# One scan per step in block 1's stick-breaking attention, and another spread of the top-k pieces of token tile 0

## The chip, the cores and the metric

The kernel runs on one core of a Trainium2 chip. The metric is the device time of one execution in microseconds. Three executions of the kernel before took 3242.63, 3243.86 and 3246.19 us; the median, 3243.86, is its time.

## What is computed

One decoder layer over 1024 tokens of width 1024, all in float32:

```
xn  = rmsnorm(x)
mix = (sigmoid(g_sb) * (stick_breaking(q, k, v) @ W_sb)
       + sigmoid(g_ml) * (mLSTM(conv_silu(q), conv_silu(k), v, i, f) @ W_ml)) @ w_out
h   = x + mix
y   = h + PEER(rmsnorm(h))
out = rmsnorm(y)
```

Stick-breaking attention has 8 heads of 64; for each query block of 128 tokens and each head it weighs all earlier keys with `w = exp(log_sigmoid(z) - suffix)`, where `suffix` is a reverse running sum of `softplus(z)` along the keys.

PEER picks, for each token and each of 8 query heads, 16 of 16384 experts: the 16 best of 128 scores in each of two halves, then the 16 best of the 256 sums. For its 128 experts a token needs the rows `u` and `v` (1024 floats each): `y = sum over experts of gate * gelu(u . x) * v`.

## The kernel before

**Blocks and tiles.** The mixer (everything up to `h`, and the expert queries and scores) works on 4 blocks of 256 tokens, b = 0 to 3. PEER works on 8 tiles of 128 tokens, i = 0 to 7; block b yields tiles 2b and 2b + 1. Block 0's mixer runs first. From then on the stream of expert rows is what the kernel is laid along.

**The stream.** Each tile has 128 experts per token, taken as 64 pairs, so there are 512 pairs (`slots`), counted on through the tiles; this text calls them pair 0 to 511. For each expert GpSimd issues one indirect DMA (`L1107`) that gathers 128 rows of `u` and `v` (8 KB a token, 1 MB in all) into one of `RS = 8` buffers of `rowsb`. VectorE takes the dot with `u` (`dot`, L1984), ScalarE the gelu (`gelu`, L1420), the gate (L1434) and a diagonal matrix (`spread`, L1439), and TensorE adds `diag * v` into `yacc` (`add_rows`, L1018, which signals `v_done`). GpSimd waits for `v_done` of the expert 8 back, that is of the pair four back, before it fills the buffer again.

**The mixer in steps.** Blocks 1 to 3 are written as Python generators, one for each engine, that are cut into the same steps: 3 of norm, 13 of the first projections (k, q, v of the attention), `n_sba(b)` of attention, 14 of the second projections (mLSTM), 29 of the mLSTM and the gates (`mix0` to `mix28`), 9 of the output, 3 of the second norm and 19 of the expert queries and scores. `steps[s][b]` says how many steps of block b follow pair s. On each engine the order in a pair s is fixed: TensorE does `add_rows`, then the steps; ScalarE `gelu`, `spread`, then the steps; VectorE the two dots, then the top-k pieces, then the steps. Each step on TensorE that projects takes one weight unit of 512 KB from a ring of three (`wt`); SyncE refills a place when TensorE has used it. The attention steps load nothing.

**The attention's steps.** A value v stands for a pair of heads and one of the two query blocks, 8 in all (`NV`), each with two heads h. `logits(v)` (TensorE, L792) makes z for both heads. `shares` (ScalarE, L1125 tanh and L1192) turns them into factors `rem`. `scan(v, h)` (VectorE, L1567 and L1570) makes the weights, `flip` (TensorE, L803) transposes them, `turn` (ScalarE, L1125) copies them to SBUF, `values(v)` (TensorE, L816) multiplies with v, and ScalarE keeps the result. Which of these a step k holds is told by `logits_at`, `scans_at`, `flips_at` and `values_at`. `sba(k)` on ScalarE does the `turn`s of the flips of step k - 1, then the `shares` of the logits of step k - 1, then keeps the y of step k. For blocks 0 and 1 (one group of keys) there are 12 steps: logits of value k, both scans and flips of value k - 2, values of k - 3. For blocks 2 and 3 (two groups) there are 20: one head's scan per step.

**Top-k.** The search for a tile's experts is cut into pieces, 9 for two heads (`top_parts`), which run on VectorE behind the dots. `parts_at[i][p]` gives the number after pair p of tile i; tile 0's last three groups and all of tile 1 are placed by the loop over n at L452 to L459. GpSimd waits for tile 0's last group of experts before it issues for pair 48, some four pairs ahead, and for those of tile 1 before pairs 64, 80, 96 and 112.

**The planner.** `steps` comes from `spread_ticks`: it goes through the pairs and places the next step of a block as long as the summed costs of TensorE, VectorE and DMA (estimates in the code, `load_of` and `slot_load`, a top-k piece at 1.75 us) don't run ahead of the time `each` of a pair, with at most two larger steps in a pair for block 1 and one for the others; `each` rises until all steps fit. Block 1's steps lie from pair 11 to pair 107. Before the change they are placed so: first projections to pair 25; `sba0` in 25, `sba1` and `sba2` in 26, then `sba3` in 27, none in 28, 4, 5, 6 in 29 to 31, none in 32, 7 and 8 in 33 and 34, none in 35, 9 to 11 in 36; second projections from 37 (`p2_1` in 38); `mix11` in 63, none in 64 and 65, `mix12` in 66; the last output steps in 89; the three norm steps in 90, 90 and 91 and the first query step in 91.

Of the kernel before, what the change touches and what calls it, by code (L numbers as in the profile page):

```python
# [66 lines left out]
def build(nc, xT, x, vecs, w_feat, w_if, w_tok, w_merge, w_out, w_query, keysT, uv, rows, out):  # L67
    ctx = ExitStack()
    with ctx:
# [203 lines left out]
        def key_groups(b):  # L273
            return (NT * b) // 4 + 1

        queries = [(hp, il) for hp in range(PAIRS) for il in range(NT)]
        NV = len(queries)


        def n_sba(b):  # L280
            return NV + 4 if key_groups(b) == 1 else 2 * NV + 4

        def logits_at(b, k):
            g_ = key_groups(b)
            return divmod(k, g_) if 0 <= k < NV * g_ else None

        def scans_at(b, k):
            if key_groups(b) == 1:
                return [(k - 2, 0), (k - 2, 1)] if 2 <= k < NV + 2 else []
            return [divmod(k - 3, 2)] if 3 <= k < 2 * NV + 3 else []  # L290

        def flips_at(b, k):
            return [(v, h, g) for v, h in scans_at(b, k) for g in range(key_groups(b))]

        def values_at(b, k):
            if key_groups(b) == 1:
                return k - 3 if 3 <= k < NV + 3 else None
            return (k - 5) // 2 if k >= 5 and k % 2 == 1 and (k - 5) // 2 < NV else None

# [8 lines left out]
        for b in range(NB):  # L308
# [7 lines left out]
            for k in range(n_sba(b)):  # L316
                if values_at(b, k) is not None:
                    put(("y", b, values_at(b, k)), own + 2)
                if logits_at(b, k):
                    for h in range(2):  # L320
                        put(("z", b) + logits_at(b, k) + (h,), own + h)
                for f, q in enumerate(flips_at(b, k)):
                    put(("flip", b) + q, own + 3 - f)
# [72 lines left out]
        def load_of(b):  # L396
            load = [(3.0, 0.0, 0.0), (5.6, 0.9, 0.0), (3.0, 0.0, 0.0)]
            load += [(UNIT_PE, 0.0, UNIT_DMA)] * len(PROJ1) + [(0.0, 0.0, 0.0)]
            for k in range(n_sba(b)):
                pe_, dve_ = 0.2, 0.2  # L400
                if logits_at(b, k):
                    pe_ += 0.9
                for v, h in scans_at(b, k):
                    dve_ += 0.3 + 3.2e-3 * (NT * b + queries[v][1] + 1) * P
                pe_ += 0.6 * len(flips_at(b, k))
                if values_at(b, k) is not None:
                    pe_ += 0.29 * (NT * b + queries[values_at(b, k)][1] + 1)
                load.append((pe_, dve_, 0.0))
# [27 lines left out]
        TOP_EACH, BLOCK_END = 9, 44  # L436
# [4 lines left out]
        N_PARTS = 4 * TOP_EACH  # L441


        parts_at = [[0] * PP for i in range(TT)]
# [7 lines left out]
        for n in range(83):  # L452
            i, p = divmod(n, PP)
            if n < 20:
                parts_at[i][p] = {0: 0, 1: 4, 2: 2, 3: 2, 4: 0, 5: 2, 6: 2, 7: 2}.get(n, 1)
            elif n < 40:
                parts_at[i][p] = (n - 19) * TOP_EACH // 20 - (n - 20) * TOP_EACH // 20
            else:
                parts_at[i][p] = (n - 39) * N_PARTS // 43 - (n - 40) * N_PARTS // 43  # L459


        def slot_load(s):
# [47 lines left out]
        with nc.Block() as block:  # L510

            @block.sync
            def _(sp):
# [45 lines left out]
                def mix(b):  # L559
# [19 lines left out]
                    for k in range(n_sba(b) if b > 0 else 0):  # L579
                        yield  # L580
# [936 lines left out]
            def _(dve):  # L1517
# [9 lines left out]
                def mix(b):  # L1527
# [45 lines left out]
                    def sba(k):  # L1573
                        if k == 0:
                            ready(dve, ("sbv", b, NT - 1))
                            mark(dve.memset(left[:, span:span + 1], 1.0))
                            settle()
                        for v, h in scans_at(b, k):
                            scan(v, h)
# [539 lines left out]
```

## Time and profile before

| | |
|---|---|
| median of three executions | 3243.86 us |
| profiled execution, its own time | 3241.54 us |
| its span | 3239.7 us |
| TensorE matmul busy | 2590.7 us (80%) |
| VectorE busy | 2075.6 us (64%) |
| ScalarE busy | 1130.4 us (35%) |
| GpSimd busy | 1209.7 us (37%) |
| DMA | 1259.44 MB, mean 389 GB/s, gathers 80.7% of 16 engines' span, weights and rest some 15% |
| granted TensorE clock, mean | 0.91 |

The page gives the span in 40 slices of 81 us, and for each the busy share of every engine, the granted clock and the DMA rate. The rate is below 285 GB/s in the first four, then between 385 and 420 in all but the last.

The chain of work that ended last goes to the gathers for 37% of the span, to TensorE for 35% and to VectorE for 10%. Matmuls are pipelined and the ends of their records are modelled, so a busy TensorE isn't one at its peak; the granted clock is 1 at 2.4 GHz and 0.5 at 1.2 GHz.

### The profile page before, as it was taken

Reading aid. Unit: us, or ns where it says so; the run is one execution under the profiler, and the core shown is the slowest. Engines: PE = TensorE matmul, PEld = TensorE weight load, DVE = VectorE, ACT = ScalarE, POOL = GpSimd, SP = SyncE. Lnnn points to the kernel's source line nnn. Section 1 sums busy time; section 2 is a strip of 40 time slices with the busy share of each in tenths; the row PEclk is TensorE's granted clock in tenths of the full one; section 3 lists DMA queues with packets and bytes.
Section 4 is the critical chain, followed back from the end, with each engine's and each line's share of the span. In section 5 each row is a group of like instructions: output and inputs, shape, how many; then the busy total and the mean of one; then the engine's idle time right before and its main releaser. Section 6 shows DMA issues by size and latency. Waiting matters only on the chain.

```text
span 3239.7 us, 40489 instructions
## 1 busy us (share of the span) xinstructions
PE 2590.7 (80%) x14564; PEld 1311.4 (40%) x14564; DVE 2075.6 (64%) x4816; ACT 1130.4 (35%) x3556; POOL 1209.7 (37%) x1048
## 2 busy tenths in 40 slices
PE   8999978998889788997787777998787555555555
PEld 6776535554455244553454333455253111111111
DVE  2325769686458887764448898775447857765444
ACT  2213345342232643332323464334222322232223
POOL 0002334333334453333334464334334443444443
PEclk9999999999999999999898999999998787777778
DMA  4467999999999999999999999999999999999998
GB/s 154 135 193 281 416 413 387 414 418 414 385 413 416 411 419 416 413 416 417 415 415 402 413 404 418 402 415 417 416 414 415 408 420 419 416 416 418 416 420 339
DMA packets 221367, 1259.44 MB, mean 389 GB/s; under 512 B 25328, under 2 KB 29424, under 8 KB 90096
## 3 DMA queue, kind: packets, MB, share of 16 engines
q0 software_dynamic: 147456, 1073.81, 80.7%
q1 hardware_dynamic: 66208, 162.61, 13.5%
q10 hardware_dynamic: 7504, 20.45, 1.6%
q8 instruction: 115, 1.88, 0.2%
q14 instruction: 84, 0.69, 0.1%
HBM read 1251.02 MB, written 5.77 MB: 388 GB/s over the span
## 4 chain that ended last, share of the span: by engine, by line
DMA 39%; PE 35%; DVE 10%; issue 6%; ACT 6%; POOL 3%; SPq 0%; POOLq 0%; DVEq 0%; ACTq 0%
DMA rowsb<-uv,e_idx 37%; PE yacc L1018 13%; PE mixp L641 8%; DVE rowsb L1984 5%; PE mixp L666 4%; POOL rowsb L1107 3%; PE mixp L748 2%; ACT diag L1439 2%; DMA wt<-w_query_ 2%; ACT wg L1434 2%; DVE area L1567 1%; PE mixp L653 1%; PE yacc L641 1%; PE mixp L677 1%; ACT gmt L1420 1%
## 5 line engine op out<-in xcount | busy, mean ns | idle before, releaser
L1107 POOL DMA_INDIRECT rowsb<-uv,e_idx x1024 | 1205.6, 1177 | 2006.8 <-PE yacc L1018 1569.2
L1984 DVE CUSTOM_DVE_ANT_0 rowsb<-rowsb,hnrow 128x1024 f32<-128x1024 f32 x1024 | 1241.8, 1222 | 835.7 <-DMA rowsb<-uv,e_idx 833.8
L1018 PE MATMUL yacc<-rowsb,diag 64*64 64x512 f32 x8176 | 1195.8, 708 | 600.6 <-ACT diag L1439 587.0
L1018 PEld LDWEIGHTS yacc<-rowsb,diag 64*64 64x64 f32 x8176 | 295.1, 149 | 1328.4 <-ACT diag L1439 903.6
L1420 ACT ACTIVATE gmt<-dots 128x2 f32<-128x2 f32 x511 | 104.0, 204 | 1575.1 <-DVE dots L1984 1574.6
L641 PE MATMUL mixp<-area,wt 128*128 128x256 f32 x2112 | 490.5, 386 | 1.8 <-DMA wt<-w_feat 1.3
L641 PEld LDWEIGHTS mixp<-area,wt 128*128 128x128 f32 x2112 | 394.1, 191 | 132.9 <-issue 82.2
L1439 ACT ACTIVATE diag<-ident,wg 128x64 f32<-128x64 f32 x1022 | 299.7, 340 | 16.7
L1434 ACT ACTIVATE wg<-gmt,gate 128x1 f32<-128x1 f32 x1022 | 245.1, 286 | 17.6
L666 PE MATMUL mixp<-area,wt 128*128 128x256 f32 x960 | 226.8, 390 | 7.1 <-DMA wt<-w_query_ 6.8
L1125 ACT ACTIVATE area<-mixp 128x512 f32<-128x512 f32 (+3 forms) x311 | 134.8, 480 | 268.8 <-PE mixp L641 156.8
L666 PEld LDWEIGHTS mixp<-area,wt 128*128 128x128 f32 x960 | 180.3, 193 | 82.8 <-issue 40.5
L748 PE MATMUL mixp<-area,wt 128*128 128x256 f32 x512 | 120.8, 391 | 3.3 <-DMA wt<-w_merge 3.3
L653 PE MATMUL mixp<-wt,area 128*128 128x512 f32 x256 | 116.9, 602 | 0.2 <-DMA wt<-w_tok 0.2
L748 PEld LDWEIGHTS mixp<-area,wt 128*128 128x128 f32 x512 | 97.9, 196 | 27.7 <-issue 7.7
L737 PE MATMUL mixp<-wt,area 128*128 128x512 f32 x192 | 91.3, 620 | 0.0
L1567 DVE TENSOR_TENSOR_SCAN area<-area 128x384 f32<-128x384 f32 (+5 forms) x48 | 78.0, 1626 | 8.7 <-ACT area L1192 7.9
L1984 DVE DVE_READ_ACCUMULATOR2_ANT dots<- 128x1 f32 x1024 | 83.5, 82 | 0.0
L653 PEld LDWEIGHTS mixp<-wt,area 128*128 128x128 f32 x256 | 46.5, 190 | 68.3 <-issue 66.3
L1420 ACT ACT_TABLE_LOAD x47 | 60.3, 1283 | 0.8
L737 PEld LDWEIGHTS mixp<-wt,area 128*128 128x128 f32 x192 | 35.6, 196 | 58.1 <-issue 58.1
L1589 DVE SCALAR_TENSOR_TENSOR area<-area,vec 128x256 f32<-128x256 f32 (+3 forms) x96 | 46.2, 481 | 6.5 <-ACT tails L1240 4.2
(305 smaller groups left out, 1831.4 us busy)
## 6 DMA issues: line engine op xcount, KB each, us to landing
wt<-w_merge SPq DMA_DIRECT2D x96, 512.0 KB, 7.9
wt<-w_feat SPq DMA_DIRECT2D x80, 512.0 KB, 7.9
wt<-w_query_ SPq DMA_DIRECT2D x62, 512.0 KB, 11.8
wt<-w_tok SPq DMA_DIRECT2D x32, 512.0 KB, 10.7
rowsb<-uv,e_idx POOLq DMA_INDIRECT x1024, 13.5
wt<-w_out_ SPq DMA_DIRECT2D x24, 512.0 KB, 8.2
rowsb<-w_out_ SPq DMA_DIRECT2D x8, 512.0 KB, 4.6
area<-keysT ACTq DMA_DIRECT2D x16, 256.0 KB, 8.2
```

What stands on the lines that cost most here:

```text
L641: last = pe.matmul(B(bank(key))[:, at:at + N], w[:, c * P:(c + 1) * P], src[:, c, :], start=c == 0, stop=c == KD - 1)
L653: last = pe.matmul(B(bank(key)), xn[:, 2 * n + c, t * P:(t + 1) * P], w[:, c * NCH:(c + 1) * NCH], start=n == 0 and c == 0, stop=n == 3 an ...
L666: last = pe.matmul(B(bank(key))[:, at:at + N], w[:, c * NCH + f * P:c * NCH + (f + 1) * P], hnT[:, 2 * m + c, :], start=m == 0 and c == 0 ...
L737: last = pe.matmul(B(bank(key)), mgT[:, n, t * P:(t + 1) * P], w[:, c * NCH:(c + 1) * NCH], start=n == 0, stop=n == KD - 1)
L748: last = pe.matmul(B(bank(key))[:, f * N:(f + 1) * N], w[:, at:at + P], src[:, c, :], start=c == 0, stop=c == 3)
L1018: last = pe.matmul(yacc[at:at + HP, k % 2, c * NCH:(c + 1) * NCH], diag[r * HP:(r + 1) * HP, s, :], rowsb[r * HP:(r + 1) * HP, s, D + c * ...
L1107: pool.indirect_dma_start(rowsb[:, n % RS, :], None, uv, bass.IndirectOffsetOnAxis(ap=e_idx[:, i % 2, k:k + 1], axis=0)).then_inc(row_load ...
L1125: act.activation(to, src, fn, **kw).then_inc(x_taken[bank(key)], 1)
L1420: act.activation(gmt[:, s:s + 2], dots[:, s:s + 2], ACT.Gelu).then_inc(gelu_done, 1)
L1434: act.activation(wg[:, s:s + 1], gmt[:, s:s + 1], ACT.Copy, scale=gate[:, i % 2, k:k + 1]).then_inc(wg_done, 1)
L1439: last = act.activation(diag[:, s, :], ident7[:, :], ACT.Copy, scale=wg[:, s:s + 1])
L1984: dve.tensor_tensor_reduce(rowsb[:, s, 0:D], rowsb[:, s, 0:D], hnrow[:, i % HR, :], 1.0, 0.0, ALU.mult, ALU.add, dots[:, s:s + 1]).then_in ...
```

## The change

Block 1 gets the 20 attention steps of blocks 2 and 3 instead of 12: in step k the logits of value k / 2 (even k only), one head's scan and flip (number k - 3), and the values at odd k from 5. Of tile 0's pairs, 20 to 25 get two top-k pieces each (12, where there were 2), 26 to 41 none (where there were 8), and from 42 on 33 pieces are spread over 41 pairs (where 35 were). The number of pieces is the same, and three of tile 1's run by pair 25. Since `slot_load` counts pieces and `load_of` counts steps, the planner places block 1's steps anew: `sba0` and `sba1` in pair 25, two steps each in 26 to 30, then `sba12` in 31, 13 and 14 in 32, 15 and 16 in 33, 17 in 34, 18 and 19 in 35; `p2_0` in 36, `p2_1` in 37 and so on, each one pair earlier than before; `mix11` in 62, `mix12` in 63; the last output steps in 88, the norm steps in 89, 89 and 90, the first query step in 91 and all later ones where they were. Blocks 2 and 3 keep their places.

```diff
         def n_sba(b):
-            return NV + 4 if key_groups(b) == 1 else 2 * NV + 4
+            return NV + 4 if b == 0 else 2 * NV + 4
 
         def logits_at(b, k):
             g_ = key_groups(b)
+            if b == 1:
+                return (k // 2, 0) if k % 2 == 0 and k < 2 * NV else None
             return divmod(k, g_) if 0 <= k < NV * g_ else None
 
         def scans_at(b, k):
-            if key_groups(b) == 1:
+            if b == 0:
                 return [(k - 2, 0), (k - 2, 1)] if 2 <= k < NV + 2 else []
             return [divmod(k - 3, 2)] if 3 <= k < 2 * NV + 3 else []
...
         def values_at(b, k):
-            if key_groups(b) == 1:
+            if b == 0:
                 return k - 3 if 3 <= k < NV + 3 else None
             return (k - 5) // 2 if k >= 5 and k % 2 == 1 and (k - 5) // 2 < NV else None
...
-            elif n < 40:
-                parts_at[i][p] = (n - 19) * TOP_EACH // 20 - (n - 20) * TOP_EACH // 20
-            else:
-                parts_at[i][p] = (n - 39) * N_PARTS // 43 - (n - 40) * N_PARTS // 43
+            elif n < 26:
+                parts_at[i][p] = 2
+            elif n >= 42:
+                parts_at[i][p] = (n - 41) * (N_PARTS - 3) // 41 - (n - 42) * (N_PARTS - 3) // 41
```

## Rows read from the trace of the kernel before

**Rows 1.** The page: GB/s moved in each of 40 slices of 81 us
```profile
GB/s 154 135 193 281 416 413 387 414 418 414 385 413 416 411 419 416 413 416 417 415 415 402 413 404 418 402 415 417 416 414 415 408 420 419 416 416 418 416 420 339
```

**Rows 2.** Windows: stretch, us; busy us (instructions) by engine; granted TensorE clock; DMA share; GB/s
```profile
376.00:444.00 68.00, 63.42 (x331) 33.77 (x329) 35.93 (x91) 18.07 (x59) 24.83 (x24) 1.00 1.02 415
...
452.00:500.00 48.00, 36.35 (x278) 16.08 (x278) 46.90 (x88) 28.32 (x83) 20.75 (x17) 0.90 0.98 399
500.00:530.00 30.00, 25.88 (x170) 13.56 (x170) 24.39 (x46) 15.36 (x46) 13.81 (x11) 0.94 0.95 357
...
600.00:650.00 50.00, 50.00 (x288) 30.61 (x288) 30.30 (x88) 15.95 (x52) 17.37 (x16) 1.00 1.02 415
...
850.00:880.00 30.00, 26.86 (x151) 16.09 (x144) 15.66 (x25) 12.52 (x36) 10.84 (x9) 0.85 0.88 334
```

**Rows 3.** Timeline of GpSimd: start us, duration, engine, line, operation [idle before, releaser]
```profile
473.38 1.13 POOL L1107 DMA_INDIRECT rowsb<-uv,e_idx  x1 [2.77 <-PE yacc L1018]
```

**Rows 4.** Timeline of VectorE, around pair 26 and around pairs 37 and 38
```profile
443.76 0.06 DVE L1576 MEMSET area<- 128x1 f32 x1 [7.07 <-PE mixp L653]
443.87 1.22 DVE L1984 CUSTOM_DVE_ANT_0 rowsb<-rowsb,hnrow 128x1024 f32<-128x1024 f32 x1
...
446.17 0.87 DVE L1903 MAX8 v<-sc 128x8 f32<-128x128 f32 x4
...
506.05 1.22 DVE L1984 CUSTOM_DVE_ANT_0 rowsb<-rowsb,hnrow 128x1024 f32<-128x1024 f32 x1
...
518.02 0.42 DVE L1600 COPY area<-mixp 4x256 f32<-4x256 f32 x1 [4.74 <-PE mixp L839]
```

**Rows 5.** Groups by line and shape, VectorE, 440 to 540: count | busy us, mean ns | idle
```profile
L1567 DVE TENSOR_TENSOR_SCAN area<-area 128x512 f32<-128x512 f32 x8 | 9.8, 1230 | 0.4
L1567 DVE TENSOR_TENSOR_SCAN area<-area 128x384 f32<-128x384 f32 x8 | 7.6, 953 | 2.6 <-ACT area L1192 2.2
L1570 DVE TENSOR_TENSOR area<-area 128x512 f32<-128x512 f32 x8 | 5.5, 692 | 0.3
L1570 DVE TENSOR_TENSOR area<-area 128x384 f32<-128x384 f32 x8 | 4.5, 564 | 0.3
```

**Rows 6.** Timeline of VectorE, an operation of a heavy top-k piece
```profile
398.53 0.69 DVE L1946 TENSOR_TENSOR sc<-v,io 128x512 f32<-128x512 f32 x1
```

**Rows 7.** Timeline of ScalarE and TensorE, pair 26
```profile
446.28 0.20 ACT L1420 ACTIVATE gmt<-dots 128x2 f32<-128x2 f32 x1 [1.48 <-DVE dots L1984]
...
447.03 0.59 ACT L1439 ACTIVATE diag<-ident,wg 128x64 f32<-128x64 f32 x2
...
447.67 1.95 PE L1018 MATMUL yacc<-rowsb,diag 64*64 64x512 f32 x16 [1.85 <-ACT diag L1439]
...
449.55 1.13 PE L792 MATMUL mixp<-keys_sb,area 64*128 64x512 f32 x4
...
450.71 1.08 ACT L1125 ACTIVATE area<-mixp 128x512 f32<-128x512 f32 x2 [1.52 <-PE mixp L792]
...
451.68 1.15 ACT L1192 ACTIVATE area<-area 128x512 f32<-128x512 f32 x2
```

**Rows 8.** Timeline of ScalarE and TensorE, 456 to 463 us
```profile
456.14 3.53 PE L1018 MATMUL yacc<-rowsb,diag 64*64 64x512 f32 x16 [2.58 <-ACT diag L1439]
...
460.52 0.28 ACT L1125 ACTIVATE area<-mixp 128x128 f32<-128x128 f32 x1 [2.10 <-PE mixp L816]
...
461.46 1.09 PE L803 MATMUL mixp<-ident,area 128*128 128x128 f32 x8
```

**Rows 9.** Timeline, a wait in the mixer, then outputs, norm and first query unit
```profile
648.19 0.84 DVE L1699 TENSOR_TENSOR area<-area,mixp 4x256 f32<-4x256 f32 x2 [5.97 <-PE mixp L914]
...
843.26 1.29 DVE L1761 SCALAR_TENSOR_TENSOR vals_sb<-mixp,vals_sb 128x512 f32<-128x512 f32 x2 [7.13 <-PE mixp L737]
...
853.12 0.17 DVE L1801 RECIPROCAL ssq<-ssq 128x2 f32<-128x2 f32 x1 [5.09 <-ACT ssq L1374]
...
868.28 1.95 POOL L1107 DMA_INDIRECT rowsb<-uv,e_idx  x1 [3.42 <-PE yacc L1018]
```

## The prediction, made before the changed kernel was built or run

> **What bounds the kernel now.** I read the page's slices first. From about 280 us to the end the kernel gathers expert rows, two per pair of slots, 512 pairs in all; the DMA rate in the slices stands near 416 GB/s almost everywhere [rows 1]. The bytes are the same before and after, so the time can only come from stretches in which the rate is lower. The slices point to two such stretches near the change, and the windows view sizes them [rows 2]: 399 GB/s over 452 to 500 us, 357 over 500 to 530, 334 over 850 to 880. Against 416 these lose 48 x (1 - 399/416) = 2.0, 30 x (1 - 357/416) = 4.3 and 30 x (1 - 334/416) = 5.9 us. The first two, 6.3 us together, are block 1's attention (the title's block 2, counted from one) and the first projections behind it. That is the ceiling of what the edit can win in its own stretch.
>
> Who starves the queue there? The gather queue on GpSimd waits for TensorE's yacc matmuls (v_done): a row buffer comes free four pairs later [rows 3]. TensorE waits for the diagonals, these for the dots. VectorE is busy 46.9 of 48 us in 452 to 500 [rows 2]: before the change VectorE sets the pace. Pair 26's dots start at 443.9, pair 37's at 506.05 [rows 4], so eleven pairs take 62.2 us. The sum of the parts agrees: a pair of dots takes 443.87 to 446.17 = 2.3 us [rows 4], eleven make 25; the 16 scans cost 0.95 and 1.23 (384 and 512 columns), their subtractions 0.56 and 0.69 [rows 5], with the gaps about 1.6 and 2.0 us, so 8 x 1.6 + 8 x 2.0 = 29; five top-k pieces make 8 or 9. Together 62 to 63.
>
> **Pieces.** The code's planner counts a piece at 1.75 us. The lightest is about its MAX8 of 0.87 [rows 4]; the heaviest holds three operations of 0.69 [rows 6] and three or four small ones, 2.9 at most. I take 1.75 and keep 0.9 to 2.9. Pairs 26 to 41 lose 8 pieces, 14 us of VectorE (7 to 23). Pairs 20 to 25 hold 12 pieces instead of 2. VectorE works 35.9 of 68 us over 376 to 444 [rows 2], and those pairs last about 6.2 us each. Two pieces (3.5 us) and the dots (2.3) make 5.8: it fits, but pairs 23 and 24, which get the heavy ends of a group, come to about 7. That puts the diagonals of pair 25 and TensorE's last sbv unit back by 0 to 3 us, I take 1.4. Pair 25's two pieces hide in the 7.07 us that VectorE waits for that unit anyway [rows 4]. If this cover were gone they would cost 3.5. Behind 42 the change places 33 pieces over 41 pairs, where there were 35; that is nothing either way. All expert indices stay tens of us ahead of GpSimd's waits (tile 0's last group is done by pair 24 instead of 39 and is wanted at 44; tile 1's groups end one pair earlier, at 49, 60 and 71, and are wanted at 60, 76 and 92). The gates stay where they were.
>
> **One scan per step.** The same 16 scans, logits, flips and values; 8 more steps. By the planner's own arithmetic the 20 steps go, two per pair, in pairs 25 to 30, then 1, 2, 2, 1, 2; they end in pair 35 instead of 36, and what follows comes one pair earlier. No instruction is added; the two heads of a value are only taken apart. What changes is the order on the in-order engines. A step 2v of a pair has logits and a flip on TensorE; the step 2v+1 in the same pair has, on ScalarE, the copy of that very flip, then the four activations of shares, then the copy of y; and only then does ScalarE reach the next pair's gelu. Before, with one step per pair, ScalarE's copies served flips of the pair before. So a turn appears: gelu to diagonals 446.28 to 447.62 = 1.34; add_rows 1.95; logits 1.13 at 512 columns, at 384 less in the ratio of the scans (0.953 to 1.230), 0.9 [rows 5, 7]; one head's flip, half of 1.09 or less, about 0.5; its copy, half of 1.08 or less, about 0.5; shares 450.71 to 452.83 = 2.1 at 512 columns, by the same ratio 1.7 at 384; y 0.28 [rows 7, 8]. Sum 1.34 + 1.95 + 1.02 + 0.5 + 0.5 + 1.9 + 0.28 = 7.5, with the handovers 7.7 us. The row that shows it in embryo is pair 26, the one that already held two steps: ScalarE waits 1.52 us for the logits of its own pair [rows 7], while in a one-step pair it goes straight on.
>
> VectorE in such a pair needs 2.3 + 1.6 + 2.0 = 6.0 us. Its second scan needs shares from ScalarE's odd step of the pair before, so it falls back to ScalarE's 7.7. Walking it through (pair: start of its dots): 27: 449, 28: 456, 29: 463, 30: 471.5, 31: 478.5, 32: 482.5, 33: 489, 34: 495.5, 35: 500, 36: 504.5, 37: 506.7. Before, 37 started at 506.05. Pairs with logits in them and two steps cost 7 to 8, the others 4 to 6.5. So the pieces' 14 us and the turn's extra cancel, and the end of attention stays where it was. In the middle it is worse: pair 30's add_rows ends near 480.5, where GpSimd's issue at 473.38 shows it at 473.1 [rows 3]; the queue runs dry for 2 to 3 us three times. At the end p2_1 waits for TensorE again: now 4.74 us [rows 4], behind add_rows and the "if" product; in my walk 5 to 7. Adding the 1.4 from the pieces, v_done is 4 to 5 us late around pair 38, with one projection unit (3.7 us, and its load) already done that was not done before. Net in this stretch: I take **+2 us**, ends -6.3 (all of the loss above recovered) and +9 (the dry queue not made good, below).
>
> **The later shift by a pair.** In the first windows of the projections and the mixer only places change. Two need a look. In 850 to 880 the same chain stays: VectorE waits 7.13 us for out7, then 5.09 for ScalarE's root [rows 9]. But qry0 now comes a pair after the last norm step, not in its pair. Before, an add_rows stood behind qry0's unit and the queue waited for it until 868.28 [rows 9]; now it goes ahead of the unit of 3.7 us, and rows are asked for up to 4 us sooner. Of the 5.9 us I take **-2** (0 to -4). The second place: mix12 follows mix11 directly, in pairs 62 and 63, where before three pairs lay between, so VectorE gets a wait like that of pair 59 (5.97 us) [rows 9] just ahead of the tile's end. TensorE is busy 50.0 of 50 us in 600 to 650 [rows 2]; it is what v_done follows there, VectorE's wait stops nothing, and the rate over that wait stayed at 415. I take 0, up to +3.
>
> **Sum.** +2 - 2 + 0 = 0 us. The profiled execution took 3241.5 us (span 3239.7), 2.3 under the median of three; a difference carries over: 3243.9 + 0, rounded 3244.
>
> **Rivals.** *A, the forecast: a ScalarE to TensorE turn takes VectorE's place* in the two-step pairs. 3239 to 3249. For it: the order of the code and the wait of 1.52 us. Against: my handovers are sums of single durations.
>
> *B, VectorE stays the bound and is relieved.* Then pairs 27 to 30 take 6.0 us each, the queue never empties, 4 to 6.3 us come back in the attention stretch and 2 to 4 later: 3234 to 3238, say 3236. For it: 46.9 busy of 48. The Trainium skill has the same rule (Perfetto Trace Analysis, Identifying the Most-Contended Engine): take the engine with the highest occupancy in the regime first. By that rule, the trace agrees for before; it doesn't say what is next, and the sum above does without it.
>
> *C, slower: the turn runs at 1.2 GHz in part.* At 456.14 one add_rows took 3.53 us instead of 1.95 after TensorE had waited 2.58 us for the diagonals [rows 8]; 452 to 500 has a mean granted clock of 0.90 [rows 2]. TensorE now lies on the turn, so each slow pair costs 1.6 (add_rows) + 1.0 (logits) + 0.5 (flip) = 3.1 us, where VectorE's pace hid it before. With three such pairs and none made good by the ring it is +9: 3253. It decides from the second slow pair on. The Trainium skill (TensorE: Matmul & The Clock Gate, Part 1: The HAM clock gate) has it that the slow clock is the default and activity lifts it; by that, waits spread over every pair would bring more slow stretches.
>
> *D, the planner gives no other order that matters* (the scans fall in the same pairs): 3244, inside A's range; its own arithmetic speaks against it.
>
> **Chances.** A 0.53, B 0.23, C 0.19, D 0.05. About 0.2% (6.5 us) is what a measurement of this kernel tells from no change. Faster by more: most of B and little of A, 0.22. Slower by more: most of C and some of A, 0.21. Between: 0.57. The range takes in most of B and C's typical value: 3235 to 3253.
>
> **What would show it.** A: in pairs 27 to 30 of the new kernel dots start 7 to 8 us apart; VectorE's scans wait for ScalarE (L1192), ScalarE's copies wait for TensorE's transposes; rate below 400 GB/s over 460 to 500. B: 6 us apart, VectorE without waits, rate 415 throughout. C: several slow-clock add_rows between 450 and 510. The -2: the window behind out8 at 360 GB/s instead of 334. The pieces: pair 26's dots at 445.3, not 443.9. The forecast fails if the turn is shorter than 6 us, or if the later shift moves more than the attention does.

## The result, and the profile of the changed kernel

The changed kernel took 3250.56 us (median of 10 runs, 3249.87 to 3255.06), the kernel before 3242.2 on the same chip (10 runs, 3240.0 to 3246.29). The ratio is 1.0025, with an interval of 1.0017 to 1.0034: 8 us slower, where 0 had been forecast, inside the range of 3235 to 3253. The profiled execution took 3250.29 us, with a span of 3248.5; before, 3241.5 and 3239.7.

The windows view of the changed kernel, over the stretches of [rows 2] and two more. Columns as there.

```profile
376.00:444.00 68.00, 63.09 (x332) 33.86 (x330) 50.89 (x155) 18.12 (x59) 29.04 (x24) 1.00 1.02 416
...
452.00:500.00 48.00, 35.32 (x275) 15.07 (x268) 38.45 (x57) 27.85 (x81) 17.68 (x15) 0.96 0.84 321
500.00:530.00 30.00, 24.45 (x170) 13.03 (x169) 19.10 (x34) 14.91 (x45) 15.71 (x12) 1.00 0.95 383
530.00:600.00 70.00, 64.91 (x348) 34.40 (x348) 55.19 (x137) 33.79 (x105) 23.91 (x22) 1.00 1.02 413
600.00:650.00 50.00, 50.00 (x288) 30.57 (x288) 32.43 (x94) 17.21 (x56) 16.47 (x16) 1.00 1.01 416
650.00:850.00 200.00, 177.38 (x940) 95.49 (x932) 135.37 (x340) 72.52 (x202) 73.08 (x62) 0.97 1.02 416
850.00:880.00 30.00, 24.12 (x137) 12.45 (x138) 15.70 (x25) 14.18 (x40) 9.28 (x10) 0.85 0.92 358
```

VectorE was busy 46.90 of 48 us in the attention stretch [rows 2] and is now busy 38.45. It was relieved, as meant, and the DMA rate fell all the same, from 399 to 321 GB/s. In time at 416 GB/s that is 48 x (399 - 321) / 416 = 9.0 us lost. The next stretch wins 30 x (383 - 357) / 416 = 1.9 back; 530 to 600 stood at 415 before and loses 0.3; 850 to 880 wins 30 x (358 - 334) / 416 = 1.7. Together 5.7 of the 8.8 us between the two spans. GpSimd's first issue for pair 50 says the same without windows; before, then in the changed kernel:

```profile
566.91 0.93 POOL L1107 DMA_INDIRECT rowsb<-uv,e_idx  x1 [2.94 <-PE yacc L1018]
```

```profile
572.70 1.33 POOL L1109 DMA_INDIRECT rowsb<-uv,e_idx  x1 [3.17 <-PE yacc L1020]
```

It comes 5.8 us later. For pair 34 it was 7.9 later (481.26 against 473.38 [rows 3]), for pair 130 it is 5.9, and for the last one, 511, 6.5 (3220.98 against 3214.48). So some 6 us are lost by pair 50 and stay lost. The other 3 us are in no place that the change touches: 1500 to 2000 us runs at 408 GB/s against 411 before (3.6 us), though nothing is placed otherwise there, and the kernels of the experiments, all with the same placing there, lie between 409 and 412; and the end behind the last pair's issue takes 2.3 us longer. I take them for the difference between one trace and another.

Why did the rate fall? These are the waits over 440 to 500 us, of before first. Columns: engine, its operation and line, the operation waited for; us in total, times, longest.

```profile
POOL rowsb L1107 <- PE yacc L1018: 35.8, 8, 7.4
PEld yacc L1018 <- ACT diag L1439: 17.2, 9, 3.2
ACT gmt L1420 <- DVE dots L1984: 14.6, 9, 3.3
```

And of the changed kernel (its lines are two further down):

```profile
POOL rowsb L1109 <- PE yacc L1020: 40.6, 8, 10.1
ACT area L1127 <- PE mixp L805: 16.0, 5, 3.4
PEld yacc L1020 <- ACT diag L1441: 14.8, 7, 3.6
...
DVE area L1569 <- ACT area L1194: 10.2, 7, 2.7
```

Before, ScalarE's gelu waited for VectorE's dots, 14.6 us in all; the changed kernel has no such wait in this stretch. In its place ScalarE's copies wait for TensorE's flips (16.0 us in 5 waits) and VectorE's scans for ScalarE's shares (10.2 us in 7); TensorE waits for ScalarE's diagonals, as before. That is a ring of two engines in which each waits for the other, while VectorE only follows. One turn of it, from ScalarE's timeline (start, duration, engine, line, operation, idle before):

```profile
462.97 0.22 ACT L1422 ACTIVATE gmt<-dots 128x2 f32<-128x2 f32 x1
...
468.07 1.57 ACT L1127 ACTIVATE area<-mixp 128x512 f32<-128x512 f32 x3 [3.26 <-PE mixp L805]
469.52 1.16 ACT L1194 ACTIVATE area<-area 128x512 f32<-128x512 f32 x2
470.56 0.29 ACT L1127 ACTIVATE area<-mixp 128x128 f32<-128x128 f32 x1
470.71 0.22 ACT L1422 ACTIVATE gmt<-dots 128x2 f32<-128x2 f32 x1
```

and TensorE's part of it:

```profile
464.38 1.95 PE L1020 MATMUL yacc<-rowsb,diag 64*64 64x512 f32 x16 [1.47 <-ACT diag L1441]
466.26 1.13 PE L794 MATMUL mixp<-keys_sb,area 64*128 64x512 f32 x4
467.32 0.66 PE L805 MATMUL mixp<-ident,area 128*128 128x128 f32 x4
```

From gelu to gelu 470.71 - 462.97 = 7.74 us. The first row of four activations covers the flip's copy and two of the shares, the second the other two. The idle 3.26 us of ScalarE are TensorE's add_rows, logits and flip; VectorE's scan of this turn, at 470.71, starts when the shares end:

```profile
470.71 1.23 DVE L1569 TENSOR_TENSOR_SCAN area<-area 128x512 f32<-128x512 f32 x1 [2.44 <-ACT area L1194]
```

GpSimd's issues show what the queue gets from it:

```profile
442.37 0.94 POOL L1109 DMA_INDIRECT rowsb<-uv,e_idx  x1 [0.30 <-issue]
453.38 1.05 POOL L1109 DMA_INDIRECT rowsb<-uv,e_idx  x1 [10.07 <-PE yacc L1020]
...
459.80 1.55 POOL L1109 DMA_INDIRECT rowsb<-uv,e_idx  x1 [4.13 <-PE yacc L1020]
...
467.13 1.29 POOL L1109 DMA_INDIRECT rowsb<-uv,e_idx  x1 [4.53 <-PE yacc L1020]
...
474.37 1.39 POOL L1109 DMA_INDIRECT rowsb<-uv,e_idx  x1 [4.70 <-PE yacc L1020]
```

A pair's two rows, of 1 MB each, are asked for every 6.4 to 7.3 us, three pairs in 474.37 - 453.38 = 21.0. The gathers move 1073.81 MB in 512 pairs (the queues' part of the page), 2.10 MB a pair, or 5.0 us at 416 GB/s; at a pair every 7.0 us the rate is 300 GB/s. Over the whole stretch 321 were measured, since the attention's last pairs are shorter.

### The profile page after: what moved, and what is told of

It reads as the page before. It is cut to its first block, busy times and chain, and to the rows that moved or that the text cites. A ratio compares the mean times of both kernels' runs of the same rounds, so it can differ in the third digit from the quotient of the medians.

```text
span 3248.5 us, 40491 instructions
## 1 busy us (share of the span) xinstructions
PE 2589.7 (80%) x14564; PEld 1307.1 (40%) x14564; DVE 2076.8 (64%) x4816; ACT 1133.9 (35%) x3558; POOL 1223.2 (38%) x1048
## 3 DMA queue, kind: packets, MB, share of 16 engines
q0 software_dynamic: 147456, 1073.81, 80.4%
## 4 chain that ended last, share of the span: by engine, by line
DMA 41%; PE 36%; DVE 7%; ACT 7%; issue 6%; POOL 4%; SPq 0%; ACTq 0%; DVEq 0%; POOLq 0%
DMA rowsb<-uv,e_idx 39%; PE yacc L1020 14%; PE mixp L643 8%; PE mixp L668 4%; POOL rowsb L1109 4%; DVE rowsb L1986 3%; ACT diag L1441 2%; PE mixp L750 2%; ACT wg L1436 2%; DMA wt<-w_query_ 2%; PE mixp L655 1%; PE yacc L643 1%; PE mixp L679 1%; ACT gmt L1422 1%; ACT area L1127 1%
## 5 line engine op out<-in xcount | busy, mean ns | idle before, releaser
L1109 POOL DMA_INDIRECT rowsb<-uv,e_idx x1024 | 1219.1, 1190 | 1999.0 <-PE yacc L1020 1558.9
```

The lines of the kernel that those rows point to most:

```text
L1109: pool.indirect_dma_start(rowsb[:, n % RS, :], None, uv, bass.IndirectOffsetOnAxis(ap=e_idx[:, i % 2, k:k + 1], axis=0)).then_inc(row_load ...
```

## The experiments

"The changed kernel" stands for the one above. In the code of the experiments `steps[n][1]` is the number of block 1's steps that follow pair n; a line that changes it comes behind the planner. Times are medians; "before" ran beside each of them, at 3241.4 to 3242.5 us. Where windows are given in one line, they are GB/s over 452 to 500, 500 to 530 and 850 to 880 us: before 399, 357, 334; the changed kernel 321, 383, 358.

### e1: odd step first

In the changed kernel pairs 26 to 30 hold steps 2v and 2v + 1. Here one step is taken out of pair 25 and comes in 26, so that pairs 26 to 31 hold 2v + 1 and 2v + 2; from 32 on nothing moves: a flip is then made in the pair ahead of the one whose copy needs it, and the logits come last. The work is the same.

```diff
+        steps[25][1] -= 1
+        steps[31][1] += 1
```

> The changed kernel with block 1's attention steps 1 to 12 paired one step later: sba0 stays in pair 25, then 1 and 2 in pair 26, 3 and 4 in 27, up to 11 and 12 in 31; from pair 32 on every step, and every top-k piece, is where the changed kernel has it. Theory (the turn between ScalarE and TensorE in pairs that hold an even step and then an odd one): in an odd-even pair the flip whose copy comes last is made without waiting for logits and shares, the turn is 5 to 6 us instead of 7.2, dots of pairs 27 to 31 start about 6 us apart, and 4 to 7 us of the 8 come back: 3244 to 3246. Rival (the extra steps, or the pieces put into pairs 20 to 25, cost the time): nothing of that is changed here, so 3249 to 3251.

Measured: 3240.6 us (11 runs), ratio 0.9993 (0.9984 to 1.0002): 10 us faster than the changed kernel, and better than either side expected. Its windows, and its waits over 440 to 500 us:

```profile
452.00:500.00 48.00, 39.83 (x326) 17.54 (x325) 45.97 (x67) 32.48 (x91) 27.02 (x19) 0.98 1.01 413
500.00:530.00 30.00, 27.13 (x170) 15.84 (x171) 18.72 (x40) 16.58 (x47) 14.84 (x11) 1.00 0.94 363
...
850.00:880.00 30.00, 27.36 (x168) 16.00 (x167) 14.80 (x27) 11.69 (x41) 13.29 (x11) 1.00 0.92 361
```

```profile
ACT area L1130 <- PE mixp L821: 6.9, 7, 2.5
...
ACT area L1130 <- PE mixp L808: 4.4, 8, 2.2
```

ScalarE's wait for the flips fell from 16.0 to 4.4 us, VectorE is busy 45.97 of 48 us again, and the rate is 413 GB/s, better than before's 399. ScalarE's gelus now start 5.4 to 6.2 us apart:

```profile
456.53 0.20 ACT L1425 ACTIVATE gmt<-dots 128x2 f32<-128x2 f32 x1
...
462.17 0.20 ACT L1425 ACTIVATE gmt<-dots 128x2 f32<-128x2 f32 x1 [0.22 <-DVE dots L1989]
...
467.58 0.20 ACT L1425 ACTIVATE gmt<-dots 128x2 f32<-128x2 f32 x1
...
473.79 0.20 ACT L1425 ACTIVATE gmt<-dots 128x2 f32<-128x2 f32 x1 [0.79 <-DVE dots L1989]
```

The one thing changed is which of two steps comes first in a pair. So the turn was what held the queue, and this run shows it. The first issue for pair 50 agrees, 9.3 us sooner than in the changed kernel:

```profile
563.39 1.63 POOL L1112 DMA_INDIRECT rowsb<-uv,e_idx  x1 [2.87 <-PE yacc L1023]
```

The Trainium skill (Perfetto Trace Analysis, Identifying the Most-Contended Engine) would have the engine with the highest occupancy optimized first. The traces agree for before and for e1 in so far as VectorE, busy 46 to 47 of 48 us, sets the pace there; in the changed kernel no engine of that stretch is busy for more than 38.45 of 48, and the pace is that of a ring, which the rule doesn't see.

### e2: the pieces alone

Block 1 keeps its twelve steps; the top-k pieces lie as in the changed kernel.

```diff
-            return NV + 4 if b == 0 else 2 * NV + 4
+            return NV + 4 if key_groups(b) == 1 else 2 * NV + 4
```

(and the same in `scans_at` and `values_at`, without the special case of `logits_at`.)

More moves than the pieces. The planner counts them, and packs the twelve steps closer: they end in pair 35, where `p2_0` now stands too (36 in the changed kernel, 37 before), and the steps behind it, up to `mix17`, come a pair or more earlier than in the changed kernel. The expectation took them for the same.

> The kernel before with the new places of the top-k pieces alone; block 1's attention keeps its 12 steps of two scans. The planner then puts later steps one pair earlier, as in the changed kernel. Theory (turn): no pair but 26 and 35 holds two attention steps, so ScalarE's copies serve flips of the pair before and VectorE, rid of 8 pieces, gains 2 to 5 us in the attention; the later shift gives 1 to 2 more: 3236 to 3240. Rival (the pieces in pairs 20 to 25 are the loss): 3247 to 3250.

Measured: 3245.15 us (11 runs), ratio 1.0011 (1.0002 to 1.002). Neither expectation held. Windows 394, 317, 342. VectorE starts pair 36's dots at 499.07 us, only 0.8 earlier than before (499.86), and then waits for the "if" product, `p2_0`'s:

```profile
508.68 0.41 DVE L1600 COPY area<-mixp 4x256 f32<-4x256 f32 x1 [7.23 <-PE mixp L839]
```

The loss sits in 500 to 530: 30 x (357 - 317) / 416 = 2.9 us. The wait is 7.23 us where it was 4.74 [rows 4]. The next pair's dots stand behind this wait on VectorE. The product is late on TensorE, where it comes behind an add_rows of 3.12 us instead of 1.95 and the last attention steps of the same pair 35; what each of these costs no run settled. 600 to 650 us also reads 408 instead of 415 GB/s, with steps placed otherwise.

### e3: the steps alone

Block 1 has its 20 steps, the top-k pieces lie as before. The planner then puts steps 2v, 2v + 1 with logits together in pairs 26, 27 and 32; pairs 29, 30 and 34 have the other order, and the attention ends in pair 36, as before. (The expectation left pair 32 out.)

```diff
-            elif n < 26:
-                parts_at[i][p] = 2
-            elif n >= 42:
-                parts_at[i][p] = (n - 41) * (N_PARTS - 3) // 41 - (n - 42) * (N_PARTS - 3) // 41
+            elif n < 40:
+                parts_at[i][p] = (n - 19) * TOP_EACH // 20 - (n - 20) * TOP_EACH // 20
+            else:
+                parts_at[i][p] = (n - 39) * N_PARTS // 43 - (n - 40) * N_PARTS // 43
```

> The kernel before with the 20 attention steps for block 1 alone; the pieces stay. The planner gives even-odd pairs only in 26 and 27 and odd-even ones from 29 on, and what follows the attention is where the kernel before has it. Theory (turn): two slow pairs instead of five, but VectorE keeps its pieces: 3243 to 3247. Rival (the number of steps costs it, wherever they lie): 3249 to 3251. Rival (the pieces cost it): 3242.

Measured: 3247.48 us (11 runs), ratio 1.0017 (1.0008 to 1.0026), half a microsecond above what was expected. Windows 390, 332, 345. It is a mixture of both orders and its time lies between those of e8 and e9 below, which have the same pieces and one order each in pairs 26 to 30.

### e4: the first query step back in its pair

The changed kernel has the norm steps in pairs 89 and 90 and the first query step in 91. Here it is in 90 again, behind a norm step.

```diff
+        steps[91][1] -= 1
+        steps[90][1] += 1
```

> The changed kernel with the first query step moved back from pair 91 into pair 90, behind the last norm step; all other steps stay. Theory: in the trace this shift won 1.6 us of DMA time between 860 and 880 us, as forecast; undone, it costs 1 to 2 us: 3251.5 to 3252.5, and the window 850 to 880 moves 335 to 345 GB/s instead of 358. Rival (the 1.6 us came from elsewhere): 3250.5.

Measured: 3250.58 us (9 runs), ratio 1.0024 (1.0014 to 1.0034), the same as the changed kernel. The window over 850 to 880 reads 353 GB/s against 358, not 335 to 345. The window says little: e5, e8 and e6, with this step where the changed kernel has it, read 344, 339 and 367. GpSimd's issues are steadier. From the first issue for pair 90 to that for pair 96 it takes 46.18 us before and 46.96 in e3, which have the norm steps in 90, 90, 91; 43.1 to 44.9 in the changed kernel, e1, e2 and e5 to e9, which have them in 89, 89, 90; and 43.49 in e4. So the later shift did win 1 to 3 us there, and it did so with the first query step in either pair.

### e5: flip ahead of the logits

In block 1's steps TensorE makes the flip first, the logits behind it: the turn would lose the logits' 0.9 or 1.1 us.

```diff
-                        if logits_at(b, k):
+                        if b != 1 and logits_at(b, k):
                             logits(*logits_at(b, k))
...
+                        if b == 1 and logits_at(b, k):
+                            logits(*logits_at(b, k))
```

> The changed kernel with TensorE's order in block 1's attention steps turned round: the flip before the logits. In an even step ScalarE's copy then waits for add_rows and one flip, no longer for the logits of 0.9 to 1.1 us. Theory (turn): the last copy and shares wait for different things that run beside each other, the turn shrinks by 0.5 us in each of five pairs (7.1 to 6.6), and the dry queue gives back 1.5 to 3 us: 3247.5 to 3249. Rival (it is the number of handovers, not their length, or VectorE): 3250.5.

Measured: 3250.1 us (11 runs), ratio 1.0022 (1.0013 to 1.0031): nothing won, as the rival had it. Windows 318, 388, 344. TensorE's timeline shows where the gain went:

```profile
450.12 3.69 PE L1022 MATMUL yacc<-rowsb,diag 64*64 64x512 f32 x16 [2.97 <-ACT diag L1443]
453.75 2.08 PE L794 MATMUL mixp<-keys_sb,area 64*128 64x512 f32 x4
...
459.25 3.64 PE L1022 MATMUL yacc<-rowsb,diag 64*64 64x512 f32 x16 [2.90 <-ACT diag L1443]
```

Two add_rows in a row were at the lower clock (granted 0.50 and 0.51), 3.69 and 3.64 us instead of 1.95, each behind an idle of 2.9 us. These first two turns took 9.1 and 8.2 us. Later, at the full clock, gelus start 7.3, 6.5 and 7.3 us apart, against 7.7, 6.9 and 7.7 in the changed kernel: 0.4 us shorter, not 1. The rest went into ScalarE's copies, which now wait for the logits: over 440 to 500 us 9.2 us for them and 11.7 for flips, 20.9 together, where the changed kernel has 5.7 and 16.0.

### e6: the order turned round from pair 28 on

```diff
+        steps[28][1] -= 1
+        steps[31][1] += 1
```

Pairs 26 and 27 keep steps 2v, 2v + 1, from 29 on the pairs hold 2v + 1, 2v + 2.

> The changed kernel with even-odd pairs kept in 26 and 27 alone: sba6 alone in pair 28, then 7 and 8 in 29, 9 and 10 in 30, 11 and 12 in 31; all else in place. Theory (each even-odd pair adds its own 1.5 us): two of the five slow pairs stay, 2 to 4 us of the 10 between the changed kernel and the odd-even one stay: 3242.5 to 3245. Rival (the first pairs, where attention starts, make the loss): nearly all stays, 3248 to 3250.

Measured: 3246.47 us (11 runs), ratio 1.001 (1.0001 to 1.0019), between the two expectations. Windows 373, 353, 367. The gelus start 9.1 and 8.4 us apart while the first order holds, 1.7 and 7.1 about the change, then 5.3 and 5.3. The turn follows the order of the steps inside one kernel; the 9.1 and 8.4 also hold slow add_rows, of 3.69 and 3.52 us. The first issue for pair 50 comes at 568.34, about midway between e1's 563.39 and the changed kernel's 572.70, and so does the time between 3240.6 and 3250.56. The time is the weaker witness: in this trace 600 to 650 us runs at 385 GB/s instead of 416, 3.7 us more, where nothing is placed otherwise.

### e7: e1 with the "if" product a pair earlier

```diff
+        steps[36][1] -= 1
+        steps[35][1] += 1
```

> The odd-even kernel with the step of the if product (p2_0) moved from pair 36 into 35, behind the last attention step; pair 36 holds no step. VectorE's wait of some 6 us for this product in pair 37 should go, since TensorE makes it a pair ahead. Theory: the queue loses 1.5 us less over 500 to 530: 3238 to 3239.5. Rival (TensorE is late anyway, so the wait and v_done stay): 3240.6.

Measured: 3241.21 us (11 runs), ratio 0.9992 (0.9983 to 1.0001), no faster than e1, as the rival had it. VectorE's wait for the product fell from 6.8 to 3.1 us, yet the rate over 500 to 530 fell too, from 363 to 354: TensorE was busy 29.83 of those 30 us. One add_rows there, at 504.50, took 3.66 us. So VectorE's wait is not what costs; that TensorE's work is, is argued from its busy time.

### e8 and e9: each order with the pieces where they were

Both have the pieces of e3 and a list of steps written out behind the planner, so that the order of the steps is that of e1 in e8 and that of the changed kernel in e9. The lists differ in pairs 25 (3 or 4 steps) and 31 (2 or 1) alone.

> The odd-even kernel with the same step in every pair but the top-k pieces where the kernel before has them: 8 more pieces in pairs 26 to 41, 10 fewer in 20 to 25. It prices the pieces' move by itself. Theory (with the short turn VectorE is again what v_done follows, 14 us of it come back in): 3 to 6 us slower than the odd-even kernel, 3243.5 to 3246.5. Rival (the pieces hide beside the turn): 3240.6.

> The changed kernel with every step in the pair where it has it (even-odd pairs 26 to 30), but the top-k pieces where the kernel before has them. With e1 and e8 it fills the square of order and pieces. In the odd-even order the pieces' move was worth 4.5 us (3245.1 against 3240.6). Theory (the slower of two sets the pace: in even-odd pairs the turn of 7 to 8 us, and VectorE's 6.0 plus one piece of 1.75 in every second pair fits beside it): the move is worth little here, 3250 to 3253. Rival (the two costs add): 3255.

Measured: e8 3245.12 us (11 runs), ratio 1.0006 (0.9997 to 1.0015), windows 391, 329, 339; e9 3251.3 us (7 runs), ratio 1.0029 (1.0018 to 1.0041). Both as the theory expected. Over 452 to 500, e9 reads

```profile
452.00:500.00 48.00, 34.47 (x269) 15.07 (x268) 40.47 (x73) 28.58 (x82) 19.08 (x16) 0.96 0.86 325
```

With e1 and the changed kernel this is a table of two by two:

| | pieces as before | pieces moved |
|---|---|---|
| steps 2v, 2v + 1 in a pair | 3251.3 (e9) | 3250.56 (changed) |
| steps 2v + 1, 2v + 2 | 3245.12 (e8) | 3240.6 (e1) |
| twelve steps, placed by the planner | 3242.2 (before) | 3245.15 (e2) |

The order costs 10.0 us with the pieces moved and 6.2 with them as before. Moving the pieces wins 4.5 us where the turn is short and 0.7, less than such medians can tell, where it is long: a relief of VectorE was worth something only where VectorE sets the pace. It isn't enough for a gain: with twelve steps VectorE sets the pace too, and there the same move, with what the planner makes of it, costs 2.6 us against the kernel before beside it (3242.52). That row isn't a clean pair.

### e10: e1 with a norm step moved behind

```diff
+        steps[89][1] -= 1
+        steps[91][1] += 1
```

> The odd-even kernel with the three norm steps of block 1 in pairs 89, 90 and 91, one each, where it has two in 89 and one in 90. VectorE's wait of 5 us for ScalarE's root, which it makes in the same pair now, falls behind the dots of a pair. Theory: of the 6 us that the queue loses over 840 to 880, 1.5 to 3 come back: 3237.5 to 3239.5. Rival (rows are late there because of the output's last unit, as e4 had it: moving steps about in these pairs changes nothing): 3240.6.

Measured: 3240.09 us (11 runs, 3234.58 to 3243.64), ratio 0.9995 (0.9986 to 1.0004). In its trace the stretch is nearly whole:

```profile
850.00:880.00 30.00, 30.00 (x184) 19.83 (x183) 12.66 (x21) 9.32 (x32) 13.44 (x12) 1.00 1.01 402
```

402 GB/s against e1's 361 is 3.0 us, and the span of this one execution, the fastest of the eleven, is 3232.8 against 3236.8. But the median of the runs moved by 0.5 us only, less than the runs differ among themselves. It is nearer to the rival's 3240.6 than to the theory's 3237.5 to 3239.5. So the stretch can be mended, and whether the kernel keeps the gain stays open. Neither e1, e7 nor e10 is clearly faster than the kernel before: each interval reaches 1 or beyond.

## Why the prediction was right where it was, and wrong where it wasn't

**The mechanism was right.** Rival A, the forecast, named the turn and its parts, and put its length at 7.7 us. Measured between gelus were 6.80 (462.97 - 456.17) and 7.74 us, in turns, with the 384 and the 512 columns; the mean is 7.3, so the length was 0.4 us too high. The copies wait for flips and the scans for ScalarE, as it said they would; e1 and e6 show that the order of the steps makes it. The walk held too: dots of pair 30 at 472.6 (forecast 471.5), 34 at 497.0 (495.5), 37 at 508.5 (506.7). Pair 30's add_rows ended at 480.96 (480.5), and 460 to 500 us ran at 302 GB/s (below 400). Only the even spacing was off: from pair 27 on dots start 8.4, 6.3, 8.1 and 6.5 us apart, not 7 to 8.

**The step that failed is the term +2.** The prediction had seen that the queue would run dry for 2 to 3 us three times in the middle, and then set the attention's net effect by its end: pieces and turn cancel, pair 37 starts where it did, so little is lost. The lateness of v_done around pair 38, forecast at 4 to 5 us, was 5.8 (add_rows at 523.72 against 517.91 before); what was wrong was to set the projection unit already done against it. That unit gave the queue nothing: at pair 50 it was still 5.8 us late. A queue that runs at 416 GB/s elsewhere, before the change as after it, doesn't catch up. Bytes not moved in 460 to 500 can only be made good in a stretch that stood below 416 before. There was one, 500 to 530 at 357 [rows 2], and it gave back 1.9 of 9.0 us. The windows over 452 to 600 sum to 9.0 - 1.9 + 0.3 = 7.4, where +2 stood, within its ends of -6.3 and +9. With 7.4 in its place and nothing else changed the forecast would have been 3243.9 + 7.4 - 2 = 3249.3. The steps were timed well; what they do to the queue was not summed.

**The range held by its width.** Rival A's own 3239 to 3249 was exceeded, and 3250.56 lies between it and C's 3253. The prediction gave 0.57 to a change of less than 6.5 us and 0.21 to a loss larger than that, and the larger loss came. (Its aside that the title counts blocks from one is a slip: block 1 is the second of 0 to 3.)

**The pieces.** Pair 26's dots were forecast at 445.3 and started at 444.6, 0.8 late where 1.4 was taken; the wait for the sbv unit fell from 7.07 to 5.12 us, which is the cover at work:

```profile
444.53 0.06 DVE L1578 MEMSET area<- 128x1 f32 x1 [5.12 <-PE mixp L655]
```

The queue stayed at 416 GB/s over 376 to 444, with VectorE busy 50.89 us instead of 35.93 [rows 2]. Twelve pieces there cost the rate nothing. What the move of the pieces was worth depends on the order of the steps: 4.5 us under e1's, 0.7 under the changed kernel's.

**The later shift.** The window behind out8 was forecast at 360 GB/s and reads 358. The sign that was named came true, but kernels with the same placing there read 339 to 367, so by itself it shows little. By the issues for pairs 90 and 96 (see e4) the -2 was right. The reason given for it, the place of qry0, was not: e4 puts it back and keeps the gain, and e3, with the norm steps left in 90, 90 and 91, hasn't got it. **mix12** was taken at 0, and 600 to 650 and 650 to 850 read 416.

**Rival B** (VectorE relieved, 3236) was wrong for this order of the steps, and near the truth for the other: e1 has 413 GB/s over 452 to 500, though its time is 3240.6, since 500 to 530 stays at 363 for TensorE's sake.

**Rival C** (the turn partly at 1.2 GHz, 3253) holds in part. Two add_rows of the changed kernel were slow in the stretch, at a granted clock of 0.54 and 0.51:

```profile
449.56 3.50 PE L1020 MATMUL yacc<-rowsb,diag 64*64 64x512 f32 x16 [2.97 <-ACT diag L1441]
...
486.75 3.62 PE L1020 MATMUL yacc<-rowsb,diag 64*64 64x512 f32 x16 [1.79 <-ACT diag L1441]
```

That is 3.50 - 1.95 and 3.62 - 1.95, 3.2 us of turn together. Before has slow ones too, 3.69 us at 494.37 and 3.40 at 511.01, beside that of [rows 8], and its mean granted clock over 452 to 500 was the lower one, 0.90 [rows 2] against 0.96; C would have it the other way. So C was not the cause of the 8 us; whether it has a share in them, beyond what before had, no run separates. In e4 a turn that held a slow add_rows (2.87 us) and slow logits (1.64 us, where 0.92 is usual) took 8.5 us instead of 6.9, so the price on the turn is real. The Trainium skill (TensorE: Matmul & The Clock Gate, Part 1: The HAM clock gate) says that the slow clock is the default and that activity lifts it. By that the slow rows should stand behind idle ones, and the trace agrees for 449.56 (2.97 us idle) and for both of e5; it doesn't for every wait, as the 2.95 us ahead of the add_rows at 457.55, which ran in 1.95. What decides between such two is not settled here.

**Open** remain how e2's loss divides between the planner's packing and the slow add_rows; the 3 us by which single traces differ where nothing is placed otherwise; and whether e10's mended window counts.

## What to carry to other kernels

Before relieving the busiest engine, lay out the order of the instructions on the others and add up each ring of two engines: the ring (7.3 us a pair here) takes the busiest engine's place as soon as that one's share (6.0 us) falls below it. Where two steps are put together, try both ways of pairing them; here the one in which a result is made in one pair and used in the next was worth 6 to 10 us, at no cost. And where a queue runs at its ceiling elsewhere, sum the time that it stands dry, not the end of the stretch: dry time is given back only in stretches that were below the ceiling before. Where a planner places the work, print its placing for each variant: here one meant to move only the top-k pieces moved steps too.

## What the runs showed of the hardware that was not expected

**GpSimd's issue of a gather can be held for the length of VectorE's dots and scans.** An issue takes 0.94 us when VectorE is idle beside it. In the changed kernel one took 4.88:

```profile
520.44 4.88 POOL L1109 DMA_INDIRECT rowsb<-uv,e_idx  x1 [3.27 <-PE yacc L1020]
525.62 0.94 POOL L1109 DMA_INDIRECT rowsb<-uv,e_idx  x1 [0.30 <-issue]
```

and VectorE's four dots of two pairs ran back to back over it:

```profile
519.86 1.21 DVE L1986 CUSTOM_DVE_ANT_0 rowsb<-rowsb,hnrow 128x1024 f32<-128x1024 f32 x1
...
521.00 1.21 DVE L1986 CUSTOM_DVE_ANT_0 rowsb<-rowsb,hnrow 128x1024 f32<-128x1024 f32 x1
...
522.15 1.21 DVE L1986 CUSTOM_DVE_ANT_0 rowsb<-rowsb,hnrow 128x1024 f32<-128x1024 f32 x1
...
523.29 1.21 DVE L1986 CUSTOM_DVE_ANT_0 rowsb<-rowsb,hnrow 128x1024 f32<-128x1024 f32 x1
```

The last of them ends at 524.50, the issue at 525.32, 0.82 us later. Nor is it the dots alone. Here a scan held one, which ended 0.75 us behind it:

```profile
1102.81 2.45 POOL L1109 DMA_INDIRECT rowsb<-uv,e_idx  x1 [0.30 <-issue]
```

```profile
1102.76 1.75 DVE L1569 TENSOR_TENSOR_SCAN area<-area 128x768 f32<-128x768 f32 x1
```

All twelve traces together show a pattern. Counted are the issues that start beside a VectorE operation with 0.3 us or more of it left. Under an operation that takes two tensors from SBUF (dots, scans, `tensor_tensor` and `scalar_tensor_tensor` with both in SBUF) 4189 of 5619 issues took longer than 0.96 us, and 4089 of these ended 0.74 to 0.83 us behind the end of that very operation. Under `tensor_tensor` and `scalar_tensor_tensor` with an operand in `mixp` or `yacc` (PSUM) none of 156 did, and under `MAX8`, `FIND_INDEX8`, `MATCH_REPLACE8` and `TENSOR_REDUCE`, which take one tensor, 9 of 936, none of them longer than 0.99. Two kinds don't fit, few as they are: reciprocals, with 9 of 21, and memsets, with all 8. The Trainium skill (SBUF — State Buffer, Who interferes with whom) has VectorE and GpSimd share a pair of ports that one instruction holds to its end, with an operation of two SBUF inputs said to block a GpSimd instruction that reads SBUF, but not the making of descriptors. The first agrees with these counts, if the issue is taken for such a reader: it reads its row numbers from `e_idx`, which lies in SBUF. That it is this read that waits, and not the descriptors, no run here shows.
